# Rotary embedding in a fused transformer kernel: the exchange of rows by transfers instead of by a matrix product

## What is computed

```python
def partial_rotary(t, pos):
    ...
    x1 = t[..., :half].astype(f32)
    x2 = t[..., half:ROT_DIM].astype(f32)
    rot = jnp.concatenate([x1 * cos - x2 * sin, x2 * cos + x1 * sin], axis=-1).astype(t.dtype)
    return jnp.concatenate([rot, t[..., ROT_DIM:]], axis=-1)
```

```python
def rotate_half(x, cos, sin):
    x1, x2 = jnp.split(x, 2, axis=-1)
    return jnp.concatenate([x1 * cos - x2 * sin, x2 * cos + x1 * sin], axis=-1)
```

## Time and profile before

| | before |
|---|---|
| time, median of 3 runs | 2769.22 us |
| profiled execution: span | 2768.6 us |
| TensorE matmuls | 2622.1 us busy (95%) |
| VectorE | 1545.5 us (56%) |
| ScalarE | 1108.5 us (40%) |
| GpSimd | 988.8 us (36%) |
| weights' queue (q1) | 259.68 MB, 26.8% of 16 DMA engines' time |

### The profile page before, as it was taken

The page is one execution under the profiler, slowest core; times in us unless marked ns, Lnnn a source line. Parts: engine busy times, 40 slices in busy tenths (PEclk is TensorE's granted clock), DMA queues, the critical chain, the costliest instruction groups (busy, mean ns, idle before and its releaser), DMA issues. The chain is left out here.

```text
span 2768.6 us, 39433 instructions
## 1 busy us (share of the span) xinstructions
PE 2622.1 (95%) x15278; PEld 2194.3 (79%) x15278; DVE 1545.5 (56%) x2406; ACT 1108.5 (40%) x2041; POOL 988.8 (36%) x571
## 2 busy tenths in 40 slices
PE   7997989899999999997999999998899997899998
PEld 5765778888888867776988888898788886788887
DVE  5454256654565355656765555656768677622324
ACT  4553442422323455555312112235555556522222
POOL 4344634445545312223323323342212212444444
PEclk9998999999999999999999999999999999999999
DMA  8633224343333100001333333311111110122222
GB/s 303 222 138 130 73 96 159 122 145 130 130 136 116 39 16 24 24 32 44 115 126 118 123 114 122 129 69 62 39 46 62 54 54 32 61 99 95 95 99 76
DMA packets 81465, 267.83 MB, mean 97 GB/s; under 512 B 8704, under 2 KB 16512, under 8 KB 81280
## 3 DMA queue, kind: packets, MB, share of 16 engines
q1 hardware_dynamic: 78944, 259.68, 26.8%
q10 hardware_dynamic: 2048, 4.33, 0.4%
q0 software_dynamic: 288, 1.31, 0.1%
HBM read 260.57 MB, written 4.72 MB: 96 GB/s over the span
## 5 line engine op out<-in xcount | busy, mean ns | idle before, releaser
L2254 POOL TENSOR_TENSOR SLO<-RAW,SHI 128x1024 fp32r<-128x1024 f32 (+1 forms) x290 | 704.9, 2433 | 1078.4 <-ACT SHI L2084 1073.0
L2084 ACT ACTIVATE SHI<-RAW 128x1024 fp32r<-128x1024 f32 (+1 forms) x334 | 344.9, 1037 | 969.6 <-PE PS L2519 967.9
L2517 PE MATMUL PS<-HLh,SHI 128*128 128x512 f32 (+1 forms) x1800 | 704.3, 391 | 11.5 <-POOL SLO L2254 5.6
L2519 PE MATMUL PS<-HLh,SLO 128*128 128x512 f32 (+1 forms) x1800 | 680.8, 378 | 0.0
L2518 PE MATMUL PS<-HLl,SHI 128*128 128x512 f32 (+1 forms) x1800 | 680.8, 378 | 0.0
L2517 PEld LDWEIGHTS PS<-HLh,SHI 128*128 128x128 f32 x1800 | 342.5, 190 | 82.6 <-issue 15.5
L2519 PEld LDWEIGHTS PS<-HLh,SLO 128*128 128x128 f32 x1800 | 341.8, 190 | 63.8
L2518 PEld LDWEIGHTS PS<-HLl,SHI 128*128 128x128 f32 x1800 | 342.7, 190 | 60.7 <-issue 5.8
L2517 PE MATMUL PS<-hh,SHI 128*128 128x512 f32 (+1 forms) x1024 | 366.2, 358 | 8.2 <-POOL SLO L2254 3.9
L2519 PE MATMUL PS<-hh,SLO 128*128 128x512 f32 (+1 forms) x1024 | 357.2, 349 | 0.0
L2518 PE MATMUL PS<-hl,SHI 128*128 128x512 f32 (+1 forms) x1024 | 355.3, 347 | 0.0
(11 more groups left out here) (261 smaller groups left out, 3944.9 us busy)
## 6 DMA issues: line engine op xcount, KB each, us to landing
RAW<-in_k_w SPq DMA_DIRECT2D x318, 512.0 KB, 3.5
ADA<-in_k_w SPq DMA_DIRECT2D x132, 512.0 KB, 4.3
early<-in_k_w SPq DMA_DIRECT2D x12, 512.0 KB, 15.1
RAW<-in_k_w SPq DMA_DIRECT2D x16, 256.0 KB, 2.6
XL<-in_xT SPq DMA_DIRECT2D x4, 512.0 KB, 8.1
bi<-in_k_bias SPq DMA_DIRECT2D x16, 128.0 KB, 4.4
out<-XL SPq DMA_DIRECT2D x16, 128.0 KB, 1.8
bi<-in_k_bias SPq DMA_DIRECT2D x8, 192.0 KB, 4.2
```

The lines of the kernel that those rows point to most:

```text
L2084: eng.activation(u.hi, u.w, ACT.Copy).then_inc(S["a_hi"], 1)
L2254: eng.tensor_tensor(u.lo, u.w, u.hi.bitcast(F32), ALU.subtract).then_inc(S["g_lo"], 1)
L2517: eng.matmul(st.out, lh, rh, start=st.first and j == 0, stop=False)
L2519: i = eng.matmul(st.out, ll, rh, start=False, stop=st.last and j == n - 1)
```

## The change

The two permutation matrices and the product with them go. In `roped`, the permuted tile is made by transfers from SBUF to SBUF instead, on the SP queue: rows of n into r2, which wait for the head norm (t_n) and for r2 to be free. With perm1 these are six per step, four of 8 rows and two of 48 (the rows that keep their place are copied too); with perm2 eight of 16 rows. A row is 512 fp32, 2 KB. All pieces of a step count on one semaphore, and VectorE's product with the sines, now in place in r2, and GpSimd's product with the cosines, which overwrites n, both wait for all of them. No bank is taken, and the step no longer counts as work in `weave`. The pieces are steps of the plan of their own, at the place where the product was.

```diff
--- before.py
+++ after.py
@@ -32,15 +32,6 @@
...
-    perm1 = np.zeros((128, 128), np.float32)
-    perm1[pi, i] = 1.0
...
-    perm2 = np.zeros((128, 128), np.float32)
-    perm2[pj, i] = 1.0
...
@@ -184,7 +175,7 @@
-HRope = namedtuple("HRope", "perm x bank r2 sin cos dst dview xview t_x t_bank t_mm t_r2free t_rope t_sin t_cos t_dfree t_done")
+HRope = namedtuple("HRope", "x r2 sin cos dst dview xview t_x t_perm t_rope t_sin t_cos t_dfree t_done")
@@ -286,7 +277,7 @@
-    CONST, _ = fixed("CONST", 640)
+    CONST, _ = fixed("CONST", 384)
@@ -297,7 +288,9 @@
-    ident, ones, bones, perm1, perm2 = (CONST[:, 128 * k:128 * k + 128] for k in range(5))
+    ident, ones, bones = (CONST[:, 128 * k:128 * k + 128] for k in range(3))
+    perm1 = [m for a in (0, 64) for m in ((a, a + 8, 8), (a + 8, a, 8), (a + 16, a + 16, 48))]
+    perm2 = [m for a in range(0, 128, 32) for m in ((a, a + 16, 16), (a + 16, a, 16))]
@@ -685,13 +678,13 @@
     def roped(n, t_n, T, perm, W, dst, t_dfree, t_rope, dview=None, xview=None):
-        b3 = take()
         r2 = W["r"].next()
-        work[0] += 4 * T
-        t6, t7, t8, t9 = tick("p_perm"), tick("v_sin"), tick("g_cos"), tick("g_rope")
-        put(HRope(perm, n.ap[:, 0:T], b3.ap[:, 0:T], r2.ap[:, 0:T], ROPE[:, 512:1024], ROPE[:, 0:512], dst,
-                          dview, xview, t_n, b3.free, t6, r2.free, t_rope, t7, t8, t_dfree, t9))
-        give(b3, t7)
+        sem = f"d_perm{W['r'].cells.index(r2)}"
+        for to, at, rows in perm:
+            t_p = dma("sp", r2.ap[to:to + rows, 0:T], n.ap[at:at + rows, 0:T], t_n, r2.free, name=sem)
+        t7, t8, t9 = tick("v_sin"), tick("g_cos"), tick("g_rope")
+        put(HRope(n.ap[:, 0:T], r2.ap[:, 0:T], ROPE[:, 512:1024], ROPE[:, 0:512], dst,
+                          dview, xview, t_n, t_p, t_rope, t7, t8, t_dfree, t9))
         n.free = [t9]
         r2.free = [t9]
         return t9
@@ -2259,7 +2252,7 @@
             def hrope(st):
-                g.wait_ge(st.t_x, st.t_mm, st.t_rope)
+                g.wait_ge(st.t_x, st.t_perm, st.t_rope)
                 eng.tensor_tensor(st.x, st.x, st.cos, ALU.mult).then_inc(S["g_cos"], 1)
@@ -2353,8 +2346,8 @@
             def hrope(st):
-                v.wait_ge(st.t_mm, st.t_r2free, st.t_rope)
-                eng.tensor_tensor(st.r2, st.bank, st.sin, ALU.mult).then_inc(S["v_sin"], 1)
+                v.wait_ge(st.t_perm, st.t_rope)
+                eng.tensor_tensor(st.r2, st.r2, st.sin, ALU.mult).then_inc(S["v_sin"], 1)
@@ -2524,10 +2517,6 @@
-            def hrope(st):
-                p.wait_ge(st.t_x, st.t_bank)
-                eng.matmul(st.bank, st.perm, st.x, start=True, stop=True).then_inc(S["p_perm"], 1)
```

More of the change, by code:

```diff
@@ L34, in shape_constants @@
     bones = (i[:, None] // 64 == i[None, :] // 64).astype(np.float32)
-    d = i % 64
-    pi = np.where(d < 8, i + 8, np.where(d < 16, i - 8, i))
-    perm1 = np.zeros((128, 128), np.float32)
-    perm1[pi, i] = 1.0
-    a = d % 32
-    pj = np.where(a < 16, i + 16, i - 16)
-    perm2 = np.zeros((128, 128), np.float32)
-    perm2[pj, i] = 1.0
     inv1 = (np.float32(500000.0) ** (-(np.arange(8, dtype=np.float32) * np.float32(2.0)) / np.float32(16))).astype(np.float32)
@@ L86, in shape_constants @@
     reset[:, ::128] = 0
-    const = np.concatenate([ident, ones, bones, perm1, perm2], 1)
+    const = np.concatenate([ident, ones, bones], 1)
     return {"k_const": const, "k_rope": np.stack([rope1, rope2]), "k_mask": masks,
@@ L2596, in hout_a @@
                 eng.matmul(st.bank, ones, st.f, start=True, stop=True).then_inc(S["p_ostat"], 1)
-            own = {Rstd: rstd_, Chunk: chunk, HNorm: hnorm, HRope: hrope, Score: score,
+            own = {Rstd: rstd_, Chunk: chunk, HNorm: hnorm, Score: score,
                    Flip: flip_, Pv: pv, DiagQ: diag_q, ScanT: scan_t, ScanO: scan_o, ScanS: scan_s,
@@ L2668, in build @@
     shapes = {"k_crow": [3, 1024], "xT": [1024, 512], "ctxT": [1024, 256], "k_cols": [128, NCOLS], "k_bias": [8, 128, 896],
-              "k_const": [128, 640], "k_rope": [2, 128, 1024], "k_reset": [128, TT],
+              "k_const": [128, 384], "k_rope": [2, 128, 1024], "k_reset": [128, TT],
               "k_mask": [128, 1536], "k_hmask": [128, 7 * 128]}
```

## The result

The changed kernel takes 2899.07 us (median of four runs, 2898.81 to 2900.35); the kernel before took 2769.29 us on the same chips (2765.15 to 2774.45). The ratio is 1.0466, with a 95% interval from 1.0452 to 1.048: 130 us slower, where 72 were forecast. The profiled execution of the changed kernel spans 2898.5 us, against 2768.6 before, so 129.9 us have to be found.

A forecast was written before the change was run, and what follows sets the result against it. The prediction took TensorE, busy 2622.1 of 2768.6 us, and whoever keeps it waiting as the bound. Its terms, 22.6 + 22 + 4 + 19.4 + 4 = 72 us, gave 2841 us, range 2780 to 2905.

The forecast's parts named there:

- the string of the second group: First block, second group: split, load's issue, pieces, cosine product and sum follow one another, 10.9 us per step instead of 7.25.
- hidden transfers: Rival: pieces land before VectorE and GpSimd come to them, so 19 + 7.7 us come off, 2742 us; chance 0.08.
- mostly absorbed holds: Rival: attention and projections absorb most holds, leaving the second group's string and half the rest, 2794 us; chance 0.20.
- that of 1.1 us per issue: Rival: each piece costs what the slowest issue rows show, 91 us on top, 2932 us; chance 0.05.
- The price of a piece: Weights' queue: 0.50 us per issue and 1.8 to land; six pieces land after 4.3 us, eight after 5.3.
- The second group: First block, last six rotary steps: sixth sum at 346.5 us against a score product at 324.50, +22 us.
- The term for the two products beside each other: Second group: sine and cosine products contend in SBUF, so each sum starts 0.7 us later, +4 us.
- The first group: First block, first six rotary steps: +7.1 for step one, +11 for two to four, +4.5 for five and six, 22.6 us.
- The second block: k0, k1 and q0 to q7: -1.7, +4.3 and 7 x 2.4 = 16.8, together +19.4 us (5 to 40).
- The slack: Second block, q1 to q7: VectorE held 3.3 us, next diagonal product has 0.9 us to spare, 2.4 us each.
- The clock: Some eight added holds of 4 to 10 us cost 0.5 us each beyond the hold, +4 us (0 to 12).
- The place in the queue: Weights' queue, first block: pieces go behind a weight load that waits for GpSimd's low split, so the waits form a chain.

The follow-up runs named there:

- the kernel with the pieces ahead: The changed kernel with each step's pieces queued right behind the head norm, not behind the weight load of the same place: 2852.65 us, ratio 1.0302.
- the best kernel here: The changed kernel with pieces right behind the head norm, two partner tiles in the first block, most rotary steps behind other VectorE work: 2804.07 us, ratio 1.0123.
- the kernel without waits: The changed kernel, its pieces copying constants to a spare tile that nobody waits for, sines multiplied with cosines, rotary values wrong: 2767.05 us, ratio 0.9993.

## Why the forecast was right, and where its terms were not

**The direction and the mechanism** held. The waits behind the transfers are the whole of the loss (2899 to 2767 us without them), the removed product is worth little beside them, and the signs that were named came, though larger: 22 idle times of VectorE before the sine product for a DMA (2.6 to 15.4 us, ten of them above the 9 named), the string of the second group (12.5 us, not 10 to 11), and more time at half clock. The rivals of hidden transfers and of mostly absorbed holds are out; so is that of 1.1 us per issue, as issues go 0.66 us apart. The misses are sizes, and the large ones are all to the same side. The time lies in the stated range, 2780 to 2905 us, but near its end, and in part by luck: the second block lost 46.9 us where the upper bound was 40, and the whole stayed inside only because other terms stayed below theirs.

**The price of a piece**, 0.50 us of issue and 1.8 to land, was 0.66 and 2.3 (0.62 and 2.0 for the eight). Six land after 5.6 us instead of 4.3, eight after 6.3 instead of 5.3. The nearest row was taken; the better one was the high bound there, 0.63 us, and it was listed. It is 1.3 us in each of 12 steps and 1.0 us in each of 10.

**The second group** was forecast at 22 + 4 and lost 34.5. The string is the forecast's with 1.3 us more for the pieces. The term for the two products beside each other was right in kind and set too high: the cosine product takes 1.71 us instead of 1.28, 0.43 us a step where 0.7 was set. Of the 12.5 us above the 22, six steps with 1.3 us more make 7.8 and six longer cosine products 2.6; the rest is about the way from the first step to the second, 15.2 us where the later ones are 12.5.

**The first group**: 37.6 instead of 22.6. The holds of VectorE were in sum those forecast (for steps two to four 9, 12 and 4 us, and VectorE was idle 10.98, 8.30 and 6.69 us; they cost 21.9 us where 11 was set), but the step that failed is the "part that TensorE hides", taken as more than half. TensorE's idle time from 160 us to the end of the group's first score products shows it: 13.6 us of 90 before, 54.4 of 128.5 after, and the clock beside it is 0.80 instead of 0.91.

```profile
160.00:250.00 90.00, 76.38 (x404) 54.20 (x403) 46.88 (x85) 36.11 (x81) 53.00 (x27) 0.91 0.43 153
```

```profile
160.00:288.50 128.50, 74.07 (x389) 54.63 (x388) 49.39 (x83) 35.83 (x80) 57.70 (x27) 0.80 0.36 119
```

Among the waits is one that I had not listed: 7.52 us for a low split of the weights, because the split is queued on GpSimd behind the cosine product that waits for the pieces. I had named the queue behind that wait and then priced VectorE's alone. Steps five and six cost 10.5 us instead of 4.5.

**The second block** was forecast at 19.4 and lost 46.9 from k0 to q7. This is the term that failed most. The hold itself was right: 3.3 us forecast, 4.17 measured, the difference being the price of a piece. The slack was wrong. I took it from the diagonal product, 6 us further on the earlier trace rows, and overlooked the residual addition, which is VectorE's next instruction behind the sine product and frees the bank for the transposes. So TensorE waits 4.8 us per tile on average from q3 to q7 (24.2 us in five places), more than the hold itself, and 6.8 us at half clock follow. Together 6.0 us per tile from q0 to q7, not 2.4. With the mixing as before it is a projection and not the transposes that waits, for the same addition and as long. The rule that I had written down, to name what is queued behind the waiting instruction, was applied to the wrong one of the queue.

**The clock**: 4 us were set, at 0.5 us per hold. Time at half level grew by 137.7 us in all. What that costs can't be split cleanly from the waits; TensorE's busy time gives an estimate: 15 us up although 19 us of products left it, 34 us. Nearly all of it lies inside the stretches above. Of the 6.5 us between the second group and k0, 4.4 are k0's own wait for its pieces (its head norm is 74.2 us behind, its cosine product 78.6), and the 4.4 us after q7 begin with q7's own wait and its 6.8 us at half clock.

**The place in the queue** was right as the cause of a third (46 us of 130 in the kernel with the pieces ahead). That behind it a wait for the partner tile stood ready, and behind that one ScalarE's wait for the sum, I had not seen.

## What to carry to other kernels

Replacing a product on TensorE of under a microsecond by transfers between SBUF rows needs other work of the engine that waits between issue and use, and even with it the best kernel here stayed 35 us behind. Look for that work in the order of that engine, not in the plan, and take the slack from its very next instruction. Count transfers, not bytes: each piece costs its issue, and at the place of a wait the issues add up. And price a hold of TensorE with the stretch at half clock that can follow it, here 6.8 us behind a wait of 5.2 us, in which like products took nearly twice as long.

## What the runs showed of the hardware

**Behind a short wait came a longer stretch at half clock.** After 7 us in which TensorE was busy 2.83 us and waited for most of the rest (5.17 us in all), the granted clock stood at half for 6.8 us, and like products started 0.43 us apart instead of 0.23. Such a stretch of 6.8 us came in each of the five query tiles q3 to q7.

**Of two instructions in SBUF, the one that started first kept its time.** In the changed kernel the sine product starts 0.11 us ahead of the cosine product: it takes its 0.69 us and GpSimd's takes 1.71 instead of 1.28. In the kernel without waits the cosine product is 0.29 us ahead: it takes 1.28 and VectorE's 1.55. Under a split VectorE's takes 1.83. The Trainium skill, "SBUF — State Buffer", on who interferes with whom and the two sides of SBUF, states this: whichever of the two starts first has the shared ports for its whole instruction. The traces agree for the start, with the numbers given; an instruction of VectorE with one SBUF tile and a scalar, 1.28 us in the same place instead of 0.48, was held as well.

**The issue of a piece does not grow with its rows.** The records of the issues are mostly 0.62 to 0.66 us for 8 rows, 0.59 for 16 and 0.54 for 48, all of 2 KB:

```profile
350.09 0.63 SPq L2050 DMA_DIRECT2D r<-f  x1
350.77 0.54 SPq L2050 DMA_DIRECT2D r<-f  x1
```

The first of these is a piece of 8 rows, the second one of 48. The Trainium skill, "DMA: Bandwidth & Descriptors", on how many engines a transfer uses, says that an 8-row copy runs on 8 engines and the sequencer writes the rest of the count. The 8-row issues are the dearest here, by 0.1 us against 48 rows; but 16 and 48 rows, which both divide by 16, differ too, by 0.05 us, so what makes the difference was not shown.
